# An expert stage rebuilt around pairs of experts: products, activation and slots of a hybrid decoder layer

## What is computed

```python
g_logits = (t @ w_router_g) + b_router_g;  g_prob = softmax(g_logits);  g_top, g_idx = top_k(g_prob, 1)
e_in = e_logits[group g_idx];  e_top, e_idx = top_k(e_in, 2)
e_w = softmax(e_top) * g_top            # combine weight of the two experts of a token
for g in range(4):                      # 4 groups of 8 experts
    a = einsum('td,edf->tef', t, w1[g]);  b = einsum('td,edf->tef', t, w3[g])
    hid = silu(a) * b * combine[:, g, :, None]
    out = out + einsum('tef,efd->td', hid, w2[g])
x = x + gate2 * out
```

## Time and profile before

| | |
|---|---|
| median of three runs | 659.46 us |
| the profiled execution | 655.55 us |
| its span, first to last instruction | 653.8 us |
| PE busy in the span | 599.4 us (92%) |
| granted clock of TensorE, mean | 0.978 |
| bytes moved by DMA | 173.85 MB, 266 GB/s over the span |

### The profile page before, as it was taken

How to read it: one execution, slowest core, us unless ns; L and a number is a source line. 1 busy time by engine, 2 the same in 40 slices (tenths; PEclk the granted TensorE clock), 3 DMA queues, 4 the chain that set the end, 5 groups by cost and what they waited for, 6 DMA issues and landing times.

```text
span 653.8 us, 7874 instructions
## 1 busy us (share of the span) xinstructions
PE 599.4 (92%) x3008; PEld 358.0 (55%) x3008; DVE 303.9 (46%) x607; ACT 168.6 (26%) x368; POOL 97.0 (15%) x136
## 2 busy tenths in 40 slices
PE   2699799999999999999999989999999988899785
PEld 0444486877676667754788745444445433344333
DVE  0228986446666564238424474322323222236167
ACT  3025022244334434242103202222223121112010
POOL 2022241079200000000001021211111111100000
PEclk9799899999999999999999999999999999899899
DMA  8994844321763306060755754899999999999963
GB/s 313 398 355 185 336 163 161 129 69 60 266 249 127 132 18 240 15 243 2 309 219 212 292 228 186 341 418 420 419 421 420 418 421 418 420 420 422 385 259 129
DMA packets 41498, 173.85 MB, mean 266 GB/s; under 512 B 6268, under 2 KB 6332, under 8 KB 28660
## 3 DMA queue, kind: packets, MB, share of 16 engines
q1 hardware_dynamic: 34128, 159.40, 61.5%
q0 software_dynamic: 5744, 12.84, 5.4%
q10 hardware_dynamic: 1588, 1.10, 0.5%
HBM read 165.36 MB, written 15.74 MB: 277 GB/s over the span
## 4 chain that ended last, share of the span: by engine, by line
PE 65%; DMA 17%; issue 6%; DVE 6%; POOL 3%; SPq 2%; ACTq 1%; ACT 1%; DVEq 0%; POOLq 0%
DMA arena<-in_w_dram 13%; PE bank L922 11%; PE bank L645 6%; PE bank L647 6%; PE bank L646 6%; PE bank L954 5%; PE bank L735 4%; POOL ss L1887 3%; DMA qkg<-in_k_norm_dram 2%; PE bank L827 2%; PE bank L937 2%; PE bank L829 2%; PE bank L828 2%; PE bank L767 2%; PE bank L669 2%
## 5 line engine op out<-in xcount | busy, mean ns | idle before, releaser
L922 PE MATMUL bank<-arena,hT 128*64 128x512 f32 x352 | 86.9, 635 | 9.2 <-DMA arena<-in_w_dram 7.9
L645 PE MATMUL bank<-hT_high,w_in_parts 128*128 128x512 f32 x160 | 66.3, 414 | 0.0
L647 PE MATMUL bank<-hT_high,w_in_parts 128*128 128x512 f32 x160 | 62.7, 392 | 0.0
L646 PE MATMUL bank<-hT_low,w_in_parts 128*128 128x512 f32 x160 | 62.4, 390 | 0.0
L922 PEld LDWEIGHTS bank<-arena,hT 128*64 128x64 f32 x352 | 24.7, 144 | 51.3 <-issue 41.8
L1206 ACT COPY probs<-bank 128x512 f32<-128x512 f32 x32 | 18.8, 587 | 120.3 <-PE bank L922 120.3
L1616 DVE TENSOR_SCALAR hT<-bank,ab 128x128 f32<-128x128 f32 x64 | 21.9, 405 | 45.4 <-PE bank L907 45.4
L954 PE MATMUL bank<-arena,g1b 128*64 128x512 f32 x176 | 39.7, 593 | 2.6 <-DVE g1b L1631 2.6
L937 PEld LDWEIGHTS bank<-fold,probs 128*128 128x128 f32 x256 | 32.6, 196 | 16.0 <-issue 11.4
L922 PE MATMUL bank<-late,hT 128*64 128x512 f32 x160 | 36.5, 598 | 3.9 <-DMA late<-in_w_dram 3.9
L1643 DVE TENSOR_TENSOR acc<-bank,g2b 128x512 f32<-128x512 f32 x18 | 11.6, 686 | 60.2 <-PE bank L954 60.2
(11 more groups left out here) (286 smaller groups left out, 999.5 us busy)
## 6 DMA issues: line engine op xcount, KB each, us to landing
arena<-in_w_dram SPq DMA_DIRECT2D x66, 1024.0 KB, 22.9
late<-in_w_dram SPq DMA_DIRECT2D x30, 1024.0 KB, 24.2
late<-in_w_ada_dram SPq DMA_DIRECT2D x6, 2048.0 KB, 12.8
arena<-in_w_ada_dram SPq DMA_DIRECT2D x5, 2048.0 KB, 8.9
arena<-in_w_in_dram SPq DMA_DIRECT2D x4, 2048.0 KB, 11.0
late<-in_w_in_dram SPq DMA_DIRECT2D x4, 2048.0 KB, 16.7
y_scratch<-arena POOLq DMA_DIRECT2D x1, 4096.0 KB, 17.7
late<-in_w_out_dram SPq DMA_DIRECT2D x2, 2048.0 KB, 7.9
```

What stands on the lines that cost most here:

```text
L645: mm(bank[:, b, :], wH[:, b, k, :], hH[:, k, :], start=k == 0, stop=False)
L646: mm(bank[:, b, :], wH[:, b, k, :], hL[:, k, :], start=False, stop=False)
L647: last = mm(bank[:, b, :], wL[:, b, k, :], hH[:, k, :], start=False, stop=k == 7)
L922: last = mm(bank[r, 2 + n % 2, :].rearrange("p (w f) -> p w f", w=2), xgT[n // 2 % 2][:, k, SLOTS * (n % 2):SLOTS * (n % 2 + 1)], w13[s][: ...
```

## The change

The expert loop runs over 16 pairs, not 32 experts. In `gate_up(q)` the two experts take the two halves of the PSUM partitions, all 8 contraction steps of an expert adding up in its own half, so there is nothing to fold: rows are slots. Tanh and the two DVE operations work there (128 x 256), and then `hidden_transposes` turns the hidden values, two transposes per pair, and ACT copies them to `hidT` for `down`.

```diff
@@ PE
+            def gate_up(q):
+                slots = [(2 * q + x) % RING for x in range(2)]
+                for s in slots:
+                    pe.wait_ge(w13_loaded[s], 32 * (2 * q // RING + 1))
...
                 for k in range(KT):
-                    r = slice(SLOTS * (k % 2), SLOTS * (k % 2 + 1))
-                    last = mm(bank[r, 2 + n % 2, :].rearrange("p (w f) -> p w f", w=2),
...
+                    for x, s in enumerate(slots):
+                        last = mm(bank[SLOTS * x:SLOTS * (x + 1), 2 + q % 2, :].rearrange("p (w f) -> p w f", w=2),
+                                  xgT[q % 2][:, k, SLOTS * x:SLOTS * (x + 1)], w13[s][:, :, k, :],
+                                  start=k == 0, stop=k == KT - 1)
+                    if q == 0 and k == 2:
+                        gather_transposes(1)
+                    if q == 0 and k in (3, 5, 6):
+                        i = 5 * ((k - 3) // 2 + k // 6)
+                        slot_sums(1, IDX_GROUPS[1][i:i + 5])
+                    if 1 <= q < PAIRS - 1 and k == 3:
+                        hidden_transposes(q - 1)
                 last.then_inc(ab_done, 1)
...
+            def step(q):
+                if q == PAIRS - 1:
+                    hidden_transposes(q - 1)
+                    down(q - 1)
+                    gate_up(q)
+                    return
+                gate_up(q)
+                if q >= 1:
+                    gather_transposes(q + 1)
+                    down(q - 1)
+                if q >= PAIRS // 2 - 2:
+                    keep_warm(4, 4 + (q - 1) % 2)
@@ SP
             def load_pair(e):
+                sp.wait_ge(ab_done, e // 2 + 1 - RING // 2)
                 for j in range(2):
-                    sp.wait_ge(ab_done, e + j + 1 - RING)
                     load13(e + j, (e + j) % RING)
...
-            sp.wait_ge(ab_done, 1)
-            load13(RING, 0)
             sp.wait_ge(idx_psum, 2)
             load2(5, 5)
...
-            for e in range(RING + 2, E, 2):
+            for e in range(RING, E, 2):
                 load_pair(e)
@@ DVE, the end
-            for t in range(2, TT):
+            for t in range(2):
                 dve.wait_ge(yg_loaded[t], 16)
                 add_stored(t)
             drain_last(1)
...
             for n in range(2 * TT):
                 t, w = n % TT, slice(CH * (n // TT), CH * (n // TT + 1))
+                if 2 <= n < TT:
+                    dve.wait_ge(yg_loaded[t], 16)
+                    add_stored(t)
                 dve.wait_ge(spread_done, n + 1)
@@ POOL
-            g.iota(iota_s, pattern=[[1, SLOTS]], base=1, **kw).then_inc(iotas_ready, 1)
+            g.iota(iota_s.rearrange("p (a b) -> p a b", b=SLOT_STEP), pattern=[[1, SLOTS // SLOT_STEP], [SLOT_STEP, SLOT_STEP]],
+                   base=1, **kw).then_inc(iotas_ready, 1)
```

More of the change, by code:

```diff
@@ L41 @@
 SLOTS = 64
+SLOT_STEP = 8
 PAIRS = E // 2
@@ L433, in overflow_blocks, with all_pairs @@
                     after()
-        def all_experts(step, before_last=None, near_end=None):
-            for n in range(E):
-                if n == E - RING and before_last:
+        def all_pairs(step, before_last=None, near_end=None):
+            for q in range(PAIRS):
+                if q == PAIRS - RING // 2 and before_last:
                     before_last()
-                if n == E - 1 and near_end:
+                if q == PAIRS - 1 and near_end:
                     near_end()
-                step(n)
-        ROWS_AT = {1: 1, 2: 2, **{n: (n + 3) // 2 for n in range(3, E - 4, 2)}}
+                step(q)
         xplace = MG.bitcast(BF16)[:, 0:2 * TT * SLOTS].rearrange("p (n s) -> p n s", s=SLOTS)
@@ L930, in fold_halves @@
[L930 to L946, removed]
+            def gate_up(q):
+                slots = [(2 * q + x) % RING for x in range(2)]
+                for s in slots:
+                    pe.wait_ge(w13_loaded[s], 32 * (2 * q // RING + 1))
+                pe.wait_ge(xgT_ready, q + 1)
+                pe.wait_ge(xgT_act, q + 1)
+                if q >= 2:
+                    pe.wait_ge(hs_ready, q - 1)
+                for k in range(KT):
+                    for x, s in enumerate(slots):
[9 more added lines that the diff above has]
+                        hidden_transposes(q - 1)
+                last.then_inc(ab_done, 1)
@@ new lines, in hidden_transposes, with down @@
+            def hidden_transposes(q):
+                pe.wait_ge(hs_ready, q + 1)
+                if q >= 2:
+                    pe.wait_ge(hid_ready, q - 1)
+                for ft in range(FT):
+                    last = nc.tensor.transpose(bank[:, 4 + q % 2, P * ft:P * (ft + 1)], hs[:, q % 2, ft:F:FT],
+                                               ident[:, :])
+                last.then_inc(hT_done, 1)
+            def down(q):
+                slots = [(2 * q + x) % RING for x in range(2)]
+                pe.wait_ge(hid_ready, q + 1)
@@ L979, in _ @@
             keep_warm(2, 5)
-            all_experts(step, near_end=lambda: counts.append(overflow_count(pe)))
-            fold_halves(E - 1)
+            all_pairs(step, near_end=lambda: counts.append(overflow_count(pe)))
             pe.wait_ge(spreadT_ready, 1)
+            hidden_transposes(PAIRS - 1)
             pe.wait_ge(yL_ready, 1)
@@ L985, in _ @@
                 spread(STORED, n)
-            down(E - 2)
+            down(PAIRS - 1)
             for n in range(4, 6):
@@ L1228, in _ @@
             modulate_gathered(0)
-            all_experts(step, near_end=near_end)
+            all_pairs(step)
+            hidden_copy(PAIRS - 1)
             for h in range(2):
@@ L1677, in near_end @@
                 counts.append(overflow_count(dve))
-                for h in range(2):
-                    y_low(0, h)
                 dve.wait_ge(tok_iota, 1)
@@ L1684, in near_end, with step @@
                 last.then_inc(spreadT_ready, 1)
-                dve.wait_ge(yg_loaded[0], 16)
-                add_stored(0)
-                dve.wait_ge(yg_loaded[1], 16)
-                add_stored(1)
-            def step(n):
-                if n == E - 2:
-                    drain_last(0)
-                elif n % 2 == 0 and n >= 2:
-                    drain_y(n // 2 - 1)
-                if n in ROWS_AT:
-                    modulate_gathered(ROWS_AT[n])
-                hidden(n)
+            def step(q):
+                if q == PAIRS - 1:
+                    drain_last(0)
+                    for h in range(2):
+                        y_low(0, h)
+                hidden(q)
+                if 1 <= q < PAIRS - 1:
+                    modulate_gathered(q + 1)
+                    drain_y(q - 1)
             dve.wait_ge(exp_out, 1)
```

105 lines of the change are left out of this document (43 added, 62 removed).

## The result

The changed kernel takes **667.86 us** (median of four runs, 667.59 to 671.09) against 658.4 us (four runs of the kernel before beside it, 654.67 to 661.25): ratio 1.0167, 95% interval 1.013 to 1.0204. It is slower by the bound of 1% that the forecast named, and 667 was the forecast. The profiled execution took 667.79 us with a span of 666.0, which is 12.2 more than the 653.8 of before.

The account below looks back on a forecast made before the run. It took weight transfers to bound the expert stage. Adding 2.4 + 4.6 + 3.5 = +10.5 us gave a span of 664.3 and execution of 666.0, or 670 against the median; it said 667 us, range 657 to 675.

Parts of the forecast that it names:

- The first rival: Gathers and scatters: the new slot ranks fall on half the DMA engines; between 661 and 675 us, chance 0.66.
- The transfers bound the stage: Expert stage: DMA busy all the time at 420 GB/s sets the pace, so a shorter PE period alone gives nothing.
- The fourth rival: PE was the bound after all in 409 to 500 us, its shorter period comes through; 648 to 652 us, chance 0.07.
- A: Stage start: the uninterrupted weight stream begins with the first `down`, which ends 2.4 us later, waiting for the third pair's gather.
- B: Weight queue on the slowest of 16 DMA engines: 5.1 us later at stream end, 4.6 at pair 14's weights.
- the count: Gather and scatter rows on the fullest DMA engine: 153 before, 191 after, at 0.172 us each, 6.5 us more.
- C: Tail from pair 14's products to the end: PE's order and later additions make the end 3.5 us later.
- S: Start of pair 14's gate and up products, when both its experts' weights are there; forecast at 612.0 us.
- The constant products lie there too: From the seventh pair, constant products cost nothing, lying under transfers of 16.6 us per pair.
- The second rival: New slots leave the DMA engines as unequal as now; 661.5 us, chance 0.14.
- The step from 670 down to 667: Final adjustment: half-clock stretches that the change takes out may be part of what lifts the median.
- Rival T: In run 9's forecast: turns between PSUM halves make products faster; 16 in one half exceed 3.65 us, nothing gained.

Follow-up runs that it names:

- 11: Changed kernel with slots dealt out, no constant products, and the first `down` ahead of the third pair's gather transposes: 654.81 us, ratio 0.9951.
- 5: Changed kernel with slots dealt out (consecutive ranks to consecutive blocks of four partitions) and the expert loop's constant products removed: 655.06 us, ratio 0.9964.
- run 1: Changed kernel with the old slot order, rank r back in slot r: 663.36 us, ratio 1.0073.
- 2: Kernel before with the changed slots alone (rank a + 8b in slot 8a + b): 664.66 us, ratio 1.0105.
- 12: Changed kernel with its own slots, without the constant products: 666.28 us, ratio 1.0142.
- 7: Changed kernel with slots dealt out and the constant products removed from pair 14's step alone: 654.07 us, ratio 0.9967.
- 4: Kernel before with slots dealt out (rank a + 8b + 32c in slot 4a + b + 32c): 651.17 us, ratio 0.9899.
- run 8: Kernel before with slots dealt out, plus three constant products ahead of expert 30's gate and up products: 651.06 us, ratio 0.9911.
- run 9: Changed kernel, slots dealt out, no constant products, each pair's experts computed one after the other from pair 1 on: 715.39 us, ratio 1.0839.

## Why the prediction was right, and where its steps were not

The first rival, slot ranks on half the engines, happened, with its sign in the place named for it. By its own steps:

**The transfers bound the stage, and a shorter PE period gives nothing: right.** PE's busy share fell to 82% in 450 to 500 us at an unchanged 420 GB/s. The fourth rival asked for 648 to 652.

**A, the first reloads: the size nearly right, one of its steps wrong.** PE waits 2.25 us for the gather (2.2 forecast). The first w2 reload is at 419.87, 26.5 us into the stage, against 23.15 before (416.19 less 393.04): 3.4 later, 2.4 forecast, mostly since the gather went out 0.4 us later in the stage than forecast and landed 0.3 slower. What A is worth is read from the bytes: at 50 us into the stage the changed kernel is 1.23 MB behind the kernel before, 2.9 us of the stream. Yet the forecast put all of it on the first `down`, and took it to cost nothing that the reload of 396.73 waits for the whole first pair. That step fails. In 11 the w2 reload goes out as early in the stage as before (23.0), and the stream is still 0.52 MB behind, 1.2 us; the five loads had landed by the first `down`, but the engines had stood idle for the 11 us ahead of them (share 0.01, against 0.49 before). And of the 3.3 us by which 11 has the w2 reload sooner than 5, only 1.0 reached the stream. That the two errors nearly cancel is luck.

**B, the slowest engine: right in kind, mis-sized.** It stood at 5.1, from 6.5 by the count and 3.8 by scaling the count to the inequality read in the earlier trace rows. Measured by itself it is 7.0 in the kernel before, and in the pair form 4.9, or 7.4 with the late stream of run 1 counted. At the point where the forecast had 4.6, expert 28's weights, 2 starts its products at 608.02, 213.8 us into the stage, and the kernel before at 599.52, 206.5 into it: 7.3. The scaling was the weak step: the fall of the ladder, 4.8 for the 8.2 of the count, understates how unequal the engines are; why it does is not shown. The rule of the Trainium skill, "DMA: Bandwidth & Descriptors", section "The descriptor swizzle", gave 6.5; the traces agree for indirect transfers too, by the four steps of the table above, and the middle that I took was worse than the rule by itself. They do not tell gathers from scatters, which the count adds up.

**C, the tail: right.** From the start S of pair 14's products the last pair's start 20.15 us later (20.2 forecast), and the end is 50.8 us after S (52.3). The clock is 1.00 from 500 us on. Only S itself was off: 221.9 us into the stage where 612.0 less 393.04 gives 219.0, 2.9 late. A is 0.5 above its 2.4, and B, if it is 7.3 at this point as in 2, 2.7 above its 4.6: 3.2, and nothing large is left open. S is also not the moment that its weights arrive, as the forecast had it. Pair 13 starts behind a wait (599.34), and from there PE's order alone, with constant products in it, makes the 15.9 us to S; without them pair 14 starts 1.1 us sooner (12: 220.8).

**"The constant products lie there too": wrong at the end.** The sum of C had them, 3.6 us in PE's order, but the part on what costs nothing named transfers of 16.6 us as their cover without saying where it ends. It ends in the tail: between pair 14's `down` and the last pair's products nothing else is waited for (20.2 against 16.6 in the forecast's own numbers), and there they cost 3 to 4 us of stage time (5, 7, 12).

**The sum.** Of the 11.9 us of stage time, slots alone make 7.0 (2) and the pair form alone 7.0 (1), of which an estimated 2.5 are the late stream of that one execution; by the ratios they make 6.9 and 4.8. Of the pair form's share with the slots dealt, 6.4 (262.2 less 255.8), the constants are 4.1. What is left, 2.3 (258.1 less 255.8), is the size of A: at 50 us into the stage 5 is 0.94 MB behind 4, 2.2 us. That fits without a price for the joint wait or for the last two experts' products behind one `down`, but no run separates these. The second rival, slots neutral at 661.5, is what run 1 made true by hand: its profiled execution is 663.04.

The span came out at 666.0 for 664.3: S 3.2 later on the clock of the trace, the part behind it 1.5 shorter. The median came out 9.5 us above the one before, for 10.5. The step from 670 down to 667, that half-clock stretches lift the median, had no row behind it. The record since leans its way: among 86 executions of the kernel before, measured beside the experiments, the 18 under 656 us have a mean granted clock of 0.979 and the 16 above 660 us one of 0.972. But the one such stretch that run 8 took out moved no median. That 667 was met within 1 us is owed in part to terms of B and C that miss in opposite directions.

## What to carry to other kernels

Where an indirect DMA skips rows, the partition that a row stands in matters: the count that gives each engine its blocks of four partitions gave the sign and, within a quarter, the size of four changes of the time (6.5, 6.5, -12.6 and -6.0 us for 7.0, 4.9, -10.5 and -5.0). Count rows per engine before changing a layout, and deal them out. Here that is one line, worth 1.0% in the kernel before and 1.5% in the changed one (1.0167 to 1.0013). Constant products that keep the clock up were free in front of a wait and cost 3.1 us where they stood ahead of products that were ready (7); look for the last such place. And compare the bytes moved at one point of a stage: they told what a late start was worth where the start itself (3.4 us) and the idle share of a few windows (0.5 us) did not.

## What the runs showed of the hardware that was not expected

Sixteen f32 products of 64 output rows and 512 columns take 3.65 us when they go to the two halves of the PSUM partitions in turn, and 7.0 to 7.1 us all in one half, at the same granted clock of 1.00. (Rival T of run 9 had named this, though no sum went by it.) The single instruction does not show it: its median is 592 ns in the changed kernel as in run 9. These are the groups of one line's instructions, count and duration as min/median/max, of the changed kernel:

```profile
L914 PE MATMUL bank<-arena,hT x352: 592/592/1061, 393.3 to 641.8; 128*64 128x512 f32 x176
```

and of 9:

```profile
L915 PE MATMUL bank<-arena,hT x352: 592/592/644, 397.1 to 691.3; 128*64 128x512 f32 x176
```

The spacing shows it: 7.04 us for 32 instructions is one every 0.22 us, 7.03 for 16 one every 0.44. In the last pair of run 9, where nothing stands between the two experts' products, the 32 take 12.24 us and not 14.1. What stays open is the cause: in run 9 successive products also add into the same place of PSUM, which those that take turns do not, and no run separates the two.
